# Layer 0's down-products from high and low parts, with one slot for the split down-weights

## The reference, cut to what matters

```
def expert_block(args):
    xblk, e = args
    return (jax.nn.silu(xblk @ w1[e]) * (xblk @ w3[e])) @ w2[e]
```

## Time and profile before

| what | us |
|---|---|
| median of 3 runs | 3174.02 |
| lowest, highest | 3169.52, 3175.81 |
| the profiled execution, its own time | 3167.55 |
| its span, first to last instruction | 3165.8 |
| TensorE busy in the span | 3051.9 (96%) |
| VectorE busy in the span | 1687.9 (53%) |
| mean granted TensorE clock | 0.985 of 2.4 GHz |

### The profile page before, as it was taken

One profiled execution on the slowest core, in us unless ns is written; L12 is line 12 of the kernel. 1 busy time (PEld: TensorE's weight loads), 2 busy tenths in 40 slices (PEclk: granted clock), 3 DMA queues, 4 the chain that ended last, 5 costly groups with the idle time before them and its releaser, 6 DMA issues. The chain is left out here.

```text
span 3165.8 us, 46392 instructions
## 1 busy us (share of the span) xinstructions
PE 3051.9 (96%) x15830; PEld 2355.7 (74%) x15831; DVE 1687.9 (53%) x2495; ACT 907.1 (29%) x1701; POOL 880.3 (28%) x530
## 2 busy tenths in 40 slices
PE   7999899999999989999999999999999998899998
PEld 4887788777777776666666888788788777666665
DVE  5473366777732677426352566366222247899540
ACT  4321365111111342222222331256111133322222
POOL 0150000111011236445554014000111112587664
PEclk9999999999999989999999999999999998999999
DMA  6122342444413447657687522242111134989753
GB/s 271 57 90 77 105 130 96 134 138 141 140 64 143 172 160 280 218 155 269 212 298 252 186 82 85 64 148 87 51 48 43 58 146 173 334 332 374 233 184 83
DMA packets 158514, 499.73 MB, mean 158 GB/s; under 512 B 30378, under 2 KB 81290, under 8 KB 135564
## 3 DMA queue, kind: packets, MB, share of 16 engines
q1 hardware_dynamic: 112008, 393.08, 33.4%
q0 software_dynamic: 17568, 59.82, 8.3%
q10 hardware_dynamic: 28804, 45.03, 4.4%
HBM read 421.76 MB, written 76.44 MB: 157 GB/s over the span
## 5 line engine op out<-in xcount | busy, mean ns | idle before, releaser
L225 PE MATMUL wide<-part,part 128*128 128x512 f32 (+2 forms) x2416 | 972.7, 403 | 25.6 <-DVEq L2910 12.6
L227 PE MATMUL wide<-part,part 128*128 128x512 f32 (+2 forms) x2416 | 926.9, 384 | 0.0
L226 PE MATMUL wide<-part,part 128*128 128x512 f32 (+2 forms) x2384 | 913.1, 383 | 0.0
L225 PEld LDWEIGHTS wide<-part,part 128*128 128x128 f32 x2416 | 456.9, 189 | 133.7 <-issue 30.8
L226 PEld LDWEIGHTS wide<-part,part 128*128 128x128 f32 x2384 | 451.4, 189 | 99.6 <-issue 18.9
L227 PEld LDWEIGHTS wide<-part,part 128*128 128x128 f32 x2416 | 456.3, 189 | 90.9
L1918 POOL TENSOR_TENSOR place<-place,place 128x512 f32 (+3 forms) x80 | 106.1, 1327 | 1063.2 <-DVE place L1860 1063.2
L2771 PE MATMUL bank<-place,place 128*128 x832 | 366.1, 593 | 5.2 <-ACT place L2860 3.7
L2904 DVE CAST part<-place 128x2048 fp32r<-128x2048 f32 x118 | 185.9, 1575 | 324.2 <-DMA place<-in_w 324.2
L2906 DVE TENSOR_TENSOR part<-place,part 128x2048 fp32r<-128x2048 f32 x118 | 339.0, 2873 | 4.0
L2771 PEld LDWEIGHTS bank<-place,place 128*128 128x128 f32 x832 | 154.0, 190 | 180.2 <-issue 180.2
(11 more groups left out here) (317 smaller groups left out, 4007.4 us busy)
## 6 DMA issues: line engine op xcount, KB each, us to landing
place<-in_w SPq DMA_DIRECT2D x116, 1024.0 KB, 4.8
place<-in_w SPq DMA_DIRECT2D x38, 2048.0 KB, 10.6
place<-in_ada_w ACTq DMA_DIRECT2D x72, 512.0 KB, 3.9
place<-in_w_gates SPq DMA_DIRECT2D x32, 640.0 KB, 4.6
place<-in_bias SPq DMA_DIRECT2D x96, 192.0 KB
place<-in_ada_w SPq DMA_DIRECT2D x6, 2048.0 KB, 17.6
place<-in_w_rows SPq DMA_DIRECT2D x6, 2048.0 KB, 15.5
place<-in_w_gates SPq DMA_DIRECT2D x16, 768.0 KB
```

The costliest lines, as they stand in the source:

```text
L225: pe.matmul(out, left[0], right[0], start=first, stop=False)
L226: pe.matmul(out, left[0], right[1], start=False, stop=False)
L227: return pe.matmul(out, left[1], right[0], start=False, stop=last)
```

## The change

In layer 0 (`last` false) the down-product becomes a product of split parts. Layer 1 keeps its code.

- `down_split`: for each column half, four `split_product`s (twelve matmuls) of `ghi`, `glo` with `down_hi`, `down_lo`.
- `copy_gated` makes two copies, `gt` and the high part `ghi`; a new GpSimd step `leave_gated` at the head of its body leaves `glo = gt - ghi`. TensorE's and ScalarE's handling of the gated rows moves ahead of that of the next rows' first half.
- w2 has one slot. `down_raw` is the old even slot; `down_lo` lies in its place, `down_hi` in the old odd slot. `load_down(e)` loads each column half (1 MB) when the down-product of the expert before it has used that half of its last block (`s_y`). VectorE splits each half, `split_down`, after the four pieces of the next expert's w13.
- At the end, w2(15) is loaded between the next layer's F and V weights, and `s_room` is raised by TensorE after the very last down-product.

```diff
+            def load_down(e, before):
+                for h in range(2):
+                    sp.wait_ge(s_y, before * 2 + (h + 1))
+                    apart(sp, s_sp)
+                    sp.dma_start(down_raw[:, :, half[h]], s["a"]["w2"][layer, e, :, :, half[h]]).then_inc(s_down[h], 16)
...
-                if e == 1:
+                if last and e == 1:
                     sp.sem_inc(s_w2[0], 16)
                     load_w2(1)
-                if e >= 3:
+                if last and e >= 3:
                     follow_w2(e - 1, older)
+                if not last and e >= 2:
+                    load_down(e - 1, before)
...
                 for i, (c, n) in enumerate(((0, F_WIDTH), (3, NAW))):
+                    if i:
+                        load_down(EXP - 1, done)
                     sp.dma_start(place(w_rows_at()[0][c], KD, n),
...
-                sp.wait_ge(s_y, done * 2 + 2)
-                sp.sem_inc(s_room, 1)
...
+            def down_split(r, b, e):
+                halves = [pe.snap(e * 2 + (h + 1)) for h in range(2)]
+                pe.wait_ge(s_glo, r * 2 + (b + 1))
+                for h in range(2):
+                    pe.wait_ge(s_dsplit, halves[h])
+                    pe.wait_ge(s_yc, r * 4 + (2 * b + h + 1))
+                    for k in range(4):
+                        mm = split_product(pe, banks[6 + h][:], (ghi[:, k, :], glo[:, k, :]),
+                                           (down_hi[:, k, half[h]], down_lo[:, k, half[h]]), k == 0, k == 3)
+                    mm.then_inc(s_y, 1)
...
-                    turn_slots(0, b, r * 2 + (b + 2))
+                    if last:
+                        turn_slots(0, b, r * 2 + (b + 2))
                     turn_gated(r, b)
+                    if not last:
+                        turn_slots(0, b, r * 2 + (b + 2))
...
             if not last:
+                pe.sem_inc(s_room, 1)
                 pe.wait_ge(s_yc, R * 4 + 4)
...
-                act.activation(gt.rearrange("p a b -> p (a b)"), banks[4][:], ACT.Copy).then_inc(s_gc, 1)
+                for to in (gt, ghi)[:COPIES]:
+                    act.activation(to.rearrange("p a b -> p (a b)"), banks[4][:], ACT.Copy).then_inc(s_gc, 1)
...
+            def split_down(e, n):
+                for h in range(2):
+                    dve.wait_ge(s_down[h], e * 16 + 16 * n)
+                    dve.tensor_copy(down_hi[:, :, half[h]], down_raw[:, :, half[h]]).then_inc(s_dhi, 1)
+                    dve.wait_ge(s_dhi, e * 2 + (2 * n + h + 1))
+                    dve.tensor_tensor(down_lo[:, :, half[h]], down_raw[:, :, half[h]],
+                                      down_hi[:, :, half[h]].bitcast(F32), ALU.subtract).then_inc(s_dsplit, 1)
...
                 for n in range(2):
                     for i in range(PIECES):
                         split_weights(e, n, i)
+                    if not last:
+                        split_down(e - 1, n)
             dve.wait_ge(s_split, (EXP + 2) * PIECES)
+            if not last:
+                split_down(EXP - 1, 0)
+                dve.wait_ge(s_dsplit, 2 * EXP)
...
+            def leave_gated(r, b):
+                pool.wait_ge(s_gc, r * 4 + (2 * b + 4))
+                pool.tensor_tensor(glo, gt, ghi.bitcast(F32), ALU.subtract).then_inc(s_glo, 1)
...
                 for b in range(2):
+                    if not last:
+                        leave_gated(r, b)
                     leave_turned(0, b, r * 2 + (b + 2))
                     gate(r * 2 + (b + 1))
```

More of the change, by code:

```diff
@@ L2606, in experts @@
     g2 = [place(at + 2 * DE, DE), place(A_W13 + 40960, DE)]
+    glo, ghi = part(at + 3 * DE, 4, P), part(at + 2 * DE, 4, P)
+    down_raw, down_lo = w2[:, 0], part(A_W13 + 32768, DE // P, D)
+    down_hi = part(A_W13 + 36864, DE // P, D)
+    half = [slice(h * 512, (h + 1) * 512) for h in range(2)]
+    COPIES = 1 if last else 2
     plan = s["plan"]
@@ L3038, in _ @@
             R = pool.snap(used // 2)
+            if not last:
+                leave_gated(R, 0)
             add_block(R, 0)
```

38 lines of the change are left out of this document (29 added, 9 removed).

## The result

| what | before | after |
|---|---|---|
| median of six runs each | 3173.66 us | 3185.79 us |
| lowest, highest | 3169.52, 3175.91 | 3183.15, 3187.30 |
| the profiled execution | 3167.55 | 3183.15 |
| layer 0's expert stage, first product to barrier | 569.56 | 583.16 |

The ratio of after to before is 1.004, with a 95% interval of 1.0029 to 1.005. The change makes the kernel 0.4% slower. I predicted 3182 us, and slower with a chance of 0.52.

What follows compares the result with a forecast made beforehand. TensorE, busy 96%, was taken as the bound. A loop gain of 5 us (39.5 saved, 34.5 in waits), 10.2 lost at the stage's end and 2.5 to the clock gave +7.7 on 3174.02: 3182 us, range 3162 to 3196.

Steps and rivals of the forecast that it cites:

- The products: Layer 0's down-product falls from 6.87 to 5.46 us, a body from 19.10 to 17.69; 28 loop bodies save 39.5 us.
- The single slot: w2's half 0 lands 2.0 us into the next body and is needed at 12.23; alone that leaves room.
- VectorE behind one-block experts: TensorE waits for w2's split: two places with one one-block expert (single), 11 us; one with two in a row (double), 14.
- The clock: In the loop, TensorE starts at the lower clock after waits of some microseconds: 3 us, bounds 0 and 8.
- The start: At the first bodies, VectorE has 12 splits before w2(1) is ready, and transfers crowd: 4 us, bounds 0 and 8.
- Low part of the next rows: GpSimd's last subtraction ends after the shorter down-product in about half the bodies: 2.5 us, bounds 0 and 8.
- The stage's end: Behind the last loop body, broadcasts start at 21.5 us, 10.2 later than before; half clock behind them adds 2.5 us.
- The rows on contention: Each GpSimd elementwise instruction costs VectorE 1.07 us as both slow; the skill's lock, 1.27, would give 3188 us in all.
- Rival 1: VectorE keeps up: a split costs 3.5 to 3.8 us, loop waits 6 to 12 us, time 3159; chance 0.20.
- rival 4: The three passes with weight loads run slower in this bank than in `up`: 3200 and more; chance 0.04.
- Rival 2: Half of it: a split at 4.0 us in VectorE's streaks, waits 22 to 28 us, time 3170; chance 0.22.
- Rival 3: Starved further: slowed GpSimd delays `glo`, low parts and gate, transfers crowd; 3 to 4 us more per one-block place, 3195; chance 0.16.

Runs made afterwards that it cites:

- b1: The kernel before with layer 0's down-product as twelve fp32r matmuls per column half, no splitting, two slots, no leave_gated: 3135.8 us, 0.9879 of before.
- x4: The changed kernel with plain four-pass float32 down-products, no splits of w2, no leave_gated; single slot and late s_room stay: 3188.6 us, 1.0052 of before.
- x2: The changed kernel without VectorE's split of w2, products taken from expert 0's high part: 3116.0 us, layer 1 routed otherwise; loop 520.18 us against 547.89.
- b2: The kernel before with only s_room moved, raised by TensorE after the very last down-product: 3182.2 us, 1.0026 of before.

## Why the prediction was right, point by point

**The products** were forecast at 5.46 us and bodies of 17.69; 17.68 was measured, and b1 gives 36.3 us for the stage.

**The single slot** was said to leave room of itself. x4 shows that: 0.5 us in the loop.

**VectorE behind one-block experts.** The step was right in place, order and cause (x2: 28 us). The forecast had two single waits of 5.4 us and 14 for the double. The rows of TensorE in after, at the two single places and in the first body of the double:

```profile
1351.17 0.79 PE L225 MATMUL bank<-part,part 128*128 128x512 f32 x1 [4.04 <-DVE part L2971]
...
1519.96 0.79 PE L225 MATMUL bank<-part,part 128*128 128x512 f32 x1 [6.51 <-DVE part L2971]
...
1650.34 0.49 PE L225 MATMUL bank<-part,part 128*128 128x512 f32 x1 [2.06 <-DVE part L2971]
...
1655.79 0.50 PE L225 MATMUL bank<-part,part 128*128 128x512 f32 x1 [2.44 <-DVE part L2971]
1656.12 0.47 PE L226 MATMUL bank<-part,part 128*128 128x512 f32 x1
1656.39 0.63 PE L227 MATMUL bank<-part,part 128*128 128x512 f32 x1
1656.82 0.63 PE L225 MATMUL bank<-part,part 128*128 128x512 f32 x1
```

The single places wait 4.0 and 6.5 us, 10.5 against 10.8. The double has waits of 2.06, 2.44, 2.6 and 2.4 for the split of w2 and 1.6 in front of the w1-product, for that of w13 (L2949): 11.1 against 14. I had put all of it in front of the down-product.

**The clock** was the term that was mis-sized: 3 us in the loop, 8 to 11.5 measured. The rows above show it. From 1656.39 on steps are 0.43 us, not 0.23, behind a wait of 2.44 us and, before that, one of 2.06; the granted clock of that body is 0.93 of 2.4 GHz, of the first one-block place 0.86. The bodies' excess over 17.68 us is 40.3 in all. 21.7 of it are the waits just named, 4.7 is block 0's, 2.4 are small excesses, the low part's among them, and the remaining 11.5 lie behind waits of 2 us and more, 1.8 to 3.2 us for each of the five bodies that have one. About 8 of these 11.5 are counted directly: some 36 steps of 0.43 in place of 0.23 us, and four first steps of 0.59 in place of 0.33. The rest lies at the edges of the waits, in the last matmul before and the first one behind each. I had taken one number for the half clock and not multiplied it by the places of my own list.

**The start** was forecast at 4 us, by VectorE and crowding transfers. It was 7.2 (6.5 in the body of block 0, which before had been 1.0 too long as well), by GpSimd, which was called hidden. TensorE never waited for VectorE's split of w2(1). GpSimd stood idle for 8.2 us ahead of its gather, for a transfer; then came the gather, an add of 3.4 us (from 1214.81), and only then `leave_gated`:

```profile
1212.38 2.13 POOL L3048 DMA_INDIRECT place<-h_rows,togather  x1 [8.21 <-DMA acc<-place,toadd]
...
1217.99 1.51 POOL L3044 TENSOR_TENSOR part<-place,part 128x512 fp32r<-128x512 f32 x1
...
1219.73 0.79 PE L225 MATMUL bank<-part,part 128*128 128x512 f32 x1 [4.66 <-POOL part L3044]
```

The step "ready near 8 to 11 us of a body" had the wait for ScalarE in it and not what is queued ahead on GpSimd.

**Low part of the next rows:** 2.5 forecast, 1.4 of waits (0.4 and 1.0). For the 34.5 us of the loop that makes 38 to 40, and the gain of 5 us was 1.1. Idle time alone was 28.1 us, where I had 31.5, and what lies beside it some 10 to 12, where I had 3. The sum was near since waits that I had too long and a clock that I had too short met. That part of the nearness is luck.

**The stage's end:** the broadcasts were forecast 21.5 us behind the loop, and came 24.5 behind it (1762.45 less 1737.92). The last down-product started at 7.8, where I had 7.2; it took 8.45 us, where I had 5.9, since its first fourteen or so matmuls ran at half clock behind 7.18 us of waiting. V's split and `scale1` took 8.3 us behind it, as forecast. The 2.5 us for the clock behind the broadcasts were 1.5 (10.74 against 9.28). In all +14.7 against +12.7.

**The rows on contention.** I took 1.07 us from VectorE for each GpSimd instruction of this kind, against the 1.27 that the Trainium skill's lock (SBUF — State Buffer, Who interferes with whom) would give. A streak of after, VectorE and GpSimd beside each other:

```profile
1341.02 1.22 DVE L2947 CAST part<-place 128x2048 fp32r<-128x2048 f32 x1
1342.06 1.32 POOL L3044 TENSOR_TENSOR part<-place,part 128x512 fp32r<-128x512 f32 x1 [2.94 <-ACT part L2900]
1342.27 3.26 DVE L2949 TENSOR_TENSOR part<-place,part 128x2048 fp32r<-128x2048 f32 x1
1343.35 3.34 POOL L3034 TENSOR_TENSOR part<-place,part 128x512 fp32r<-128x512 f32 x1
1345.46 2.32 DVE L2969 CAST part<-place 128x2048 fp32r<-128x2048 f32 x1
...
1348.86 3.31 POOL L3034 TENSOR_TENSOR part<-place,part 128x512 fp32r<-128x512 f32 x1
```

The subtraction is 0.97 longer than alone (2.29), the cast 1.10 (1.22), each by one GpSimd instruction. GpSimd pays as well, 3.34 us for what takes 1.27. The ends of the rows tell how: GpSimd's L3034 ends at 1346.69, 1.16 us behind VectorE's subtraction (1345.53), and the cast ends at 1347.78, 1.09 behind L3034. So the two take turns, a whole instruction each, and the waiting is inside the durations; they don't both run at a lower speed, as my forecast had it. Where GpSimd has several instructions ready, VectorE doesn't get between them. This is beside block 0's down-product:

```profile
1217.88 7.46 DVE L2949 TENSOR_TENSOR part<-place,part 128x2048 fp32r<-128x2048 f32 x1
...
1219.21 1.52 POOL L3034 TENSOR_TENSOR part<-place,part 128x512 fp32r<-128x512 f32 x1
1220.43 1.52 POOL L3040 TENSOR_TENSOR place<-place,place 128x512 f32<-128x512 f32 x1
1221.66 1.52 POOL L3034 TENSOR_TENSOR part<-place,part 128x512 fp32r<-128x512 f32 x1
```

With the one from 1217.99 these are four GpSimd instructions, 1.22 us apart, and the subtraction is 5.17 us longer than alone, 1.29 for each. The trace thus agrees with the lock that I had set aside. Its price is 0.97 to 1.10 us in a streak, as my rows had it, and 1.27 or so where VectorE is kept out for several.

VectorE's busy time rose by 151 us, not by 125. The 32 splits of w2, at 1.22 and 2.29 us alone, are 112 of them; so some 39 are turns of GpSimd's, where 125 would leave 13. The 30 casts and 30 subtractions of the loop and the end took 49.9 and 83.2 us, expert 0's two splits 8.1, and the splits of w13 10.6 more than before. The column half of w2, 4 x 512, is cast in 1.21 us where GpSimd is idle (1745.49), as fast as a piece of w13, as the Trainium skill's rule (VectorE: DVE Perf Modes, What auto-detection actually checks) had it.

**The sum and the rivals.** +7.7 us was forecast on the median and +12 measured (3173.66 to 3185.79), inside the range. The stage in the trace gives +13.6. Rival 1, that VectorE keeps up, is refuted by the streaks, rival 4 by b1. Rival 2 had waits of 22 to 28 us and 3170: idle time in the loop was 28.1 us, and what its time left out is the clock behind the waits. Rival 3 was partly right: GpSimd, slowed itself, did delay `glo`, but once, at the start.

## What to carry to other kernels

Before work is moved from the engine that is the bound to one that is half idle, add up that engine's work over the shortest stretch between two deadlines (here a one-block expert, six splits in 17.7 us), with what a neighbour on the same memory takes from it; the mean share of busy time says nothing on this. To every body with a wait of some microseconds add what the wait and TensorE's clock cost besides, 1.8 to 3.2 us here. And look at the end of a stage apart from its loop: here a release moved by one down-product cost some 9 us, and nearly all of it (8.7) came back when two instructions of 0.2 us were moved ahead in VectorE's order.

## What the hardware showed that was not expected

- TensorE's clock: a wait of 2.06 us, until 1650.34, left it at full clock, while the next, of 2.44 us until 1655.79, was followed by 3.4 us at half. Before, a wait of 2.67 us at the stage's end had left it at full clock; b2 has the same 2.67 us and a product of 8.83 in place of 7.13 us behind it. Why the same wait leads to both isn't known from these runs.
- VectorE and GpSimd: on these instructions they take turns, a whole instruction each. VectorE loses 0.97 to 1.10 us to one GpSimd subtraction, or 1.29 each to four in a row (7.46 us in place of 2.29); GpSimd's 1.27 become as much as 3.34 us. A duration in the profile has this waiting in it.
- A load of a column half of w2, 1 MB in rows of 512 floats, took 5.5 us from its issue (1735.45) to VectorE's cast (1740.97), against 4.7 from issue to landing for a piece of w13. The two ends aren't the same, and a gather of rows ran beside the load of w2 (1735.64), so that no cause is shown.
